# Two down projections as seven products of halves, with weight sums made in HBM and token sums made on VectorE

## The reference, cut to what matters

```python
def conv_ffn(x, w_up, conv_w, conv_b, w_down):      # x: (1, 512, 1024), D_FF = 2816
    up = x @ w_up
    a, g = up[..., :D_FF], up[..., D_FF:]
    g = causal_dwconv(g, conv_w) + conv_b
    return (jax.nn.gelu(g) * a) @ w_down             # (512 x 2816) @ (2816 x 1024)
...
x = layer_norm(alpha * x + conv_ffn(...), ln_ffn_g[layer], ln_ffn_b[layer])
```

## Time and profile before

| what | value |
|---|---|
| median of 3 runs | 1785.68 us (1784.17 to 1785.85) |
| profiled execution | 1786.04 us |
| its span, first to last instruction | 1784.2 us |
| PE busy | 1758.9 us, 99% of the span |
| PEld (weight loads, beside PE) | 1472.9 us, 83% |
| DVE busy | 1027.2 us, 58% |
| ACT busy | 652.2 us, 37% |
| POOL busy | 99.5 us, 6% |
| mean granted TensorE clock | 0.998 of full |
| HBM traffic | 189.67 MB, mean 106 GB/s |

### The profile page before, as it was taken

How to read it: one execution, slowest core, us unless ns; L and a number is a source line. 1 busy time by engine, 2 the same in 40 slices (tenths; PEclk the granted TensorE clock), 3 DMA queues, 4 the chain that set the end, 5 groups by cost and what they waited for, 6 DMA issues and landing times.

```text
span 1784.2 us, 27491 instructions
## 1 busy us (share of the span) xinstructions
PE 1758.9 (99%) x11571; PEld 1472.9 (83%) x11571; DVE 1027.2 (58%) x1480; ACT 652.2 (37%) x1013; POOL 99.5 (6%) x136
## 2 busy tenths in 40 slices
...
GB/s 302 111 94 113 113 49 77 147 95 102 98 95 107 94 83 128 109 95 117 108 107 60 89 195 153 142 154 130 138 94 36 151 60 73 38 38 63 176 36 83
DMA packets 146010, 189.67 MB, mean 106 GB/s; under 512 B 7800, under 2 KB 95092, under 8 KB 145120
## 3 DMA queue, kind: packets, MB, share of 16 engines
...
HBM read 181.58 MB, written 6.30 MB: 105 GB/s over the span
## 4 chain that ended last, share of the span: by engine, by line
PE 93%; DVE 4%; issue 1%; ACT 1%; POOL 1%; DMA 0%; SPq 0%; DVEq 0%; ACTq 0%
PE ps L329 28%; PE ps L331 27%; PE ps L330 27%; PE ps L970 2%; PE ps L518 1%; PE ps L2222 1%; PE ps L2242 1%; PE ps L1628 1%; PE ps L2236 1%; PE ps L2256 0%; DVE LATE L2303 0%; PE ps L2359 0%; PE ps L982 0%; DVE WL L313 0%; PE ps L1652 0%
## 5 line engine op out<-in xcount | busy, mean ns | idle before, releaser
L313 DVE TENSOR_TENSOR WL<-RAW,WH 128x1024 fp32r<-128x1024 f32 x289 | 350.8, 1223 | 501.3 <-ACT WH L303 500.0
L329 PE MATMUL ps<-XH,WH 128*128 128x512 f32 (+1 forms) x1416 | 524.6, 371 | 3.4 <-DVE XL L1498 1.6
L303 ACT ACTIVATE WH<-RAW 128x1024 fp32r<-128x1024 f32 x289 | 303.5, 1058 | 597.5 <-PE ps L331 570.0
L331 PE MATMUL ps<-XH,WL 128*128 128x512 f32 (+1 forms) x1416 | 518.2, 366 | 0.0
L330 PE MATMUL ps<-XL,WH 128*128 128x512 f32 (+1 forms) x1416 | 517.9, 366 | 0.0
L329 PE MATMUL ps<-WH,XH 128*128 128x512 f32 x784 | 312.7, 399 | 2.4 <-DVE WL L313 1.1
L329 PEld LDWEIGHTS ps<-XH,WH 128*128 128x128 f32 x1416 | 267.5, 189 | 51.4 <-issue 6.1
L331 PE MATMUL ps<-WH,XL 128*128 128x512 f32 x784 | 305.8, 390 | 0.0
L330 PE MATMUL ps<-WL,XH 128*128 128x512 f32 x784 | 305.5, 390 | 0.0
L331 PEld LDWEIGHTS ps<-XH,WL 128*128 128x128 f32 x1416 | 267.4, 189 | 43.4
L330 PEld LDWEIGHTS ps<-XL,WH 128*128 128x128 f32 x1416 | 267.7, 189 | 40.9
...
## 6 DMA issues: line engine op xcount, KB each, us to landing
RAW<-ffn_w_up SPq DMA_DIRECT2D x176, 256.0 KB, 3.2
RAW<-ffn_w_down SPq DMA_DIRECT2D x44, 512.0 KB, 3.7
RAW<-w_in SPq DMA_DIRECT2D x33, 512.0 KB, 3.9
RAW<-xa_wkv SPq DMA_DIRECT2D x32, 512.0 KB, 3.8
RAW<-c_w_in SPq DMA_DIRECT2D x24, 512.0 KB, 3.8
LATE<-w_ada SPq DMA_DIRECT2D x24, 512.0 KB, 4.8
RAW<-xa_wq SPq DMA_DIRECT2D x16, 512.0 KB, 5.7
RAW<-xa_wo SPq DMA_DIRECT2D x16, 512.0 KB, 3.7
```

The source lines that it names most:

```text
L303: e.activation(halves_of(i)[0][:, :, 0:w], raw(i)[:, :, 0:w], ACT.Copy).then_inc(*w_hi.up(i))
L313: e.tensor_tensor(wl[:, :, 0:w], raw(i)[:, :, 0:w], wh[:, :, 0:w].bitcast(F), ALU.subtract).then_inc(*w_lo.up(i))
L329: e.matmul(o, lh, rh, start=start, stop=False)
L331: return e.matmul(o, ll, rh, start=False, stop=stop)
```

## The change

With the features and the tokens cut in halves, the down projection is a product of 2 x 2 blocks. A11 and A21 are tokens 0 to 255 and 256 to 511 of features 0 to 1407, A12 and A22 the same of features 1408 to 2815; B00, B01, B10, B11 are the blocks of `w_down`. Strassen's scheme in Winograd's form makes it seven products of 256 x 1408 by 1408 x 512:

- product 1: A11 by B00; product 2: A12 by B10
- product 3: (A12 + s2) by B11; product 4: A22 by t4
- product 5: s1 by t1; product 6: s2 by t2; product 7: s3 by t3
- s1 = A21 - A22, s2 = s1 - A11, s3 = A11 - A21
- t1 = B00 + B01, t3 = B01 + B11, t2 = t3 + B00, t4 = t2 + B10, up to signs that are put right when the products are added

**Weight sums.** t1 to t4 of each layer are made in HBM (`d_sum`) by DMAs that POOL issues in `sums_pool`: for each sum a copy from HBM to HBM and then an accumulating DMA, each in two parts (6 and 5 feature tiles). Steps 0 to 5 are placed between stages: layer 0's step 0 before the four norms of the gating branch in `ab_pool`, then one step before and one behind the norms of "mix" and of "xa" in each layer, and step 5 before those of "ffn"; layer 1's step 0 follows layer 0's last norm.

**Token sums.** `token_sums` on DVE makes s3, s1 (in place of A21), s2 and A12 + s2 of each of 11 feature tiles, four operations of 128 x 256; nine of the eleven are inside the up projection, two in the down projection. `token_out` (POOL) writes s3, s2 and A12 + s2 to HBM (`d_tok`), and `token_in` (POOL) brings them back as needed into `ring`, two places of 128 x 512. A reload waits until the low part of the item two loads before it has been made.

**The order of the down projection.** 39 chunks and 40 token "items" of 128 x 512 per layer. Chunks 0 to 21 alternate a, a, b, b: a holds B00 and t1 (products 1 and 5), b holds t2 and t3 (products 6 and 7). Chunks 22 to 32 hold B10 and B11 (products 2 and 3), chunks 33 to 38 hold t4 (product 4). Items A are tiles of A11 with s1, B of s3 and s2, C of A12, D of A12 + s2, E of A22; B and D come through `ring`. Two 128-token tiles u = 0, 1 per product. Products 1, 5, 6 and 7 hold all eight PSUM banks; products 2 and 3 take the four banks of 1 and 5. DVE and ACT combine the products into `XR` in steps 20 to 28, and do the norm rows behind step 32. `early_pool` now stands behind `down_pool` on POOL's queue. The code, cut to its core:

```diff
+FAST = [(name, q + i) for q in range(0, 11, 2) for name in "ab" for i in range(min(2, 11 - q))]
+FAST += [("c", k) for k in range(11)] + [("e", q) for q in range(6)]
+def pair(q):
+    return min(2, 11 - 2 * q)
+def w_fast(l):
+    first["ffn", l] = len(chunks)
+    w = I["ffn_w_down"][l]
+    for name, k in FAST:
+        if name == "a":
+            chunks.append(([((0, 1), 512, w[128 * k:128 * k + 128, 0:512].unsqueeze(1)),
+                            ((1, 2), 512, d_sum[l][k][:, 2:3, :])], 512, ("t1", l, k)))
+        if name == "b":
+            chunks.append(([((0, 2), 512, d_sum[l][k][:, 0:2, :])], 512, ("t3", l, k)))
+        if name == "c":
+            chunks.append(([((0, 2), 512, w[1408 + 128 * k:1536 + 128 * k, :].rearrange("p (k n) -> p k n", k=2))],
+                           512, None))
+        if name == "e":
+            v = d_sum[l][2 * k:2 * k + pair(k)]
+            chunks.append(([((0, pair(k)), 512, v[:, :, 3, :].rearrange("k p n -> p k n"))], 512, ("t4", l, 2 * k + pair(k) - 1)))
...
+        if chunks[i][2] is not None:
+            what, l, k = chunks[i][2]
+            for name in (("t2", "t3") if what == "t3" else (what,)):
+                e.wait_ge(*sum_in[name][k // 6].at(l))
...
+        if nb == 9:
+            item_lo(e, l, 0)
+            item_lo(e, l, 1)
+        if nb > 6:
+            token_sums(e, l, 2 * nb - 13)
+        for c in range(4 if nb else 0):
+            if nb > 5 and c == 2:
+                token_sums(e, l, 2 * nb - 12)
+            if l:
+                side()
+            lo_to(e, first["up", l, nb] + min(c + 1, 3 if nb == 10 else 4) + NH)
+            if l:
+                side()
+        if nb < 10:
+            lo_to(e, first["up", l, nb] + 4 + NH)
+            for i in range(2):
+                conv_dve(e, l, nb, i)
+                gated_dve(e, l, nb, i)
+    conv_dve(e, l, 10, 0)
+    item_lo(e, l, 2)
+    conv_dve(e, l, 10, 1)
+    item_lo(e, l, 3)
+    gated_dve(e, l, 10, 0)
+    gated_dve(e, l, 10, 1)
+    lo_to(e, first["up", l, 10] + 4 + NH)
...
+    a11, a21, a12, a22 = hT[:, k, 0:256], hT[:, k, 256:512], hT[:, 11 + k, 0:256], hT[:, 11 + k, 256:512]
...
+    e.wait_ge(*ffn_v.at(("h", l, 11 + k)))
+    e.tensor_tensor(s3, a11, a21, ALU.subtract).then_inc(*ffn_v.up())
+    e.wait_ge(*latest["V"])
+    e.tensor_tensor(a21, a21, a22, ALU.subtract).then_inc(*ffn_v.up(("s1", l, k)))
+    e.wait_ge(*latest["V"])
+    e.tensor_tensor(s2, a21, a11, ALU.subtract).then_inc(*ffn_v.up())
+    e.wait_ge(*latest["V"])
+    e.tensor_tensor(last, a12, s2, ALU.add).then_inc(*ffn_v.up(("s", l, k)))
...
+    def part(name, g):
+        return d_sum[l][6 * g:6 + 5 * g, :, place[name], :].rearrange("k p n -> p k n")
+    def block(r, c, g):
+        return w[1408 * r + 768 * g:1408 * r + 768 + 640 * g, 512 * c:512 * c + 512].rearrange("(k p) n -> p k n", p=P)
+    def copied(name, g, src):
+        e.dma_start(part(name, g), src).then_inc(*sum_in[name][g].up((l, "copy")))
+    def added(name, g, src):
+        e.wait_ge(*sum_in[name][g].at((l, "copy")))
+        e.dma_start(part(name, g), src, accum_op=ALU.add).then_inc(*sum_in[name][g].up(l))
+    for g in range(2):
+        if step == 0:
+            copied("t1", g, block(0, 1, g))
+            copied("t3", g, block(0, 1, g))
+        if step == 1:
+            added("t1", g, block(0, 0, g))
+            added("t3", g, block(1, 1, g))
+        if step == 2:
+            e.wait_ge(*sum_in["t3"][g].at(l))
+            copied("t2", g, part("t3", g))
+        if step == 3:
+            added("t2", g, block(0, 0, g))
+        if step == 4:
+            e.wait_ge(*sum_in["t2"][g].at(l))
+            copied("t4", g, part("t2", g))
+        if step == 5:
+            added("t4", g, block(1, 0, g))
...
+def down_pool(e, l):
+    for i in range(2, 17):
+        token_in(e, l, i)
+        if i == 3:
+            token_out(e, l, 9)
+        if i == 7:
+            token_out(e, l, 10)
...
+def items_at(s):
+    got = [s + 8] if s < 14 else []
+    got += [ITEMS.index(("C", q)) for q, at in enumerate((2, 6, 10, 13, 16, 18)) if at == s]
+    got += [ITEMS.index(("D", q)) for q in range(6) if 14 + q == s]
+    return got + [ITEMS.index(("E", q)) for q, at in enumerate((20, 21, 23, 25, 27, 29)) if at == s]
...
 def down_pe(e, l):
...
+    for s, (name, k) in enumerate(ITEMS[0:22]):
+        e.wait_ge(*w_lo.at(i0 + s))
+        ready(s)
+        of = ((1, 0), (5, 256)) if name == "A" else ((6, 256), (7, 0))
+        for half, (p, at) in enumerate(of):
+            for u in range(2):
+                key = ("down", l, p, u)
+                if k == 0:
+                    ps.take(key)
+                    for w in ps.vacant(key):
+                        e.wait_ge(*w)
+                r = product(key, s, at + 128 * u, i0 + s, half, k == 0, k == 10)
...
+    for k in range(11):
+        i, mc = i0 + 22 + k, 22 + 2 * (k // 2)
+        e.wait_ge(*w_lo.at(i))
+        for half, p in enumerate((2, 3)):
...
+    for q in range(2):
+        for u in range(2):
+            last(q, u)
+    for u in range(2):
+        for q in range(2, 6):
+            last(q, u)
+            if (u, q) in ((0, 5), (1, 3)):
+                behind(u)
...
 def down_dve(e, l):
...
+    def row(t):
+        u = t % 2
+        if t < 2:
+            e.wait_ge(*gemm.at(("down", l, 2, u)))
+            e.wait_ge(*ln_v.at((n, "x11", u)))
+            add(2, t, 0)
+            stats_of(t, 0)
+            e.wait_ge(*gemm.at(("down", l, 3, u)))
+            e.wait_ge(*ln_v.at((n, "x12", u)))
+            add(3, t, 1)
+            stats_of(t, 1)
...
+    for s in range(33):
+        for u in range(2):
+            if s == 20:
+                e.wait_ge(*dn_a.at(("u", l, u)))
+                scaled(u, 0, U[u]).then_inc(*ln_v.up((n, "x11", u)))
+            if s == 21:
+                e.wait_ge(*gemm.at(("down", l, 6, u)))
+                e.wait_ge(*ln_v.at((n, "x11", u)))
+                e.tensor_tensor(U[u], U[u], ps.tile(("down", l, 6, u))[:, :], ALU.add).then_inc(
+                    *ps.empties(("down", l, 6, u), ln_v, (n, "sum", u)))
+                e.wait_ge(*ln_v.at((n, "sum", u)))
+                e.wait_ge(*gemm.at(("down", l, 5, u)))
+                e.tensor_tensor(Y[u], ps.tile(("down", l, 5, u))[:, :], U[u], ALU.subtract).then_inc(
+                    *ps.empties(("down", l, 5, u), ln_v, (n, "y", u)))
...
+        lo_to(e, min(i0 + s + 1 + NH, limit))
+        if s == 1:
+            token_sums(e, l, 9)
+        if s == 5:
+            token_sums(e, l, 10)
+        for m in items_at(s):
+            item_lo(e, l, m)
     for t in range(4):
+        if l == 0 and t == 2:
+            turn_dve(e, n, 0)
+        if l == 0 and t == 3:
+            lo_to(e, i0 + 36 + NH)
+        row(t)
+        if l == 0 and t == 2:
+            turn_dve(e, n, 1)
+        if l == 0 and t == 3:
+            lo_to(e, i0 + 37 + NH)
+        row_end(t)
+        if t < 2:
+            lo_to(e, min(i0 + 34 + t + NH, limit))
...
 def gpsimd(e):
...
+            if name == "mix":
+                sums_pool(e, l, 1)
+            if name == "xa":
+                sums_pool(e, l, 3)
+            if name == "ffn":
+                sums_pool(e, l, 5)
+                tokens_pool(e, l)
+                down_pool(e, l)
             if (name, l) == ("ffn", 1):
                 early_pool(e)
...
```

More of the change, by code:

```diff
@@ L245, in programs @@
             w_values(1, 0)
-        for b in range(2):
-            w_block(("ffn", l, b), I["ffn_w_down"][l], 512 * b, rows=DFF)
+        w_fast(l)
     for name, c0, n in (("k", 512, 512), ("w", 2048, 128), ("r", 0, 512), ("v", 1024, 512), ("aq", 2176, 512),
@@ L289, in programs @@
     c_a = sig("c_act", "A")
+    sum_in = {name: [sig(f"sum_{name}{g}", "dma", 16) for g in range(2)] for name in ("t1", "t2", "t3", "t4")}
+    tok_out, tok_in = sig("tok_out", "dma", 16), [sig(f"tok_in{i}", "dma", 16) for i in range(2)]
+    dn_a = sig("dn_a", "A")
     made = {"hi": 0, "lo": 0, "w": 0}
@@ new lines, in gated_dve @@
+    def gated_dve(e, l, nb, i):
+        j = 2 * nb + i
+        e.wait_ge(*ffn_a.at(("gelu", l, j)))
+        e.tensor_tensor(hT[:, j, :], gc[i], ps.tile((("up", l, nb), i))[:, :], ALU.mult).then_inc(
+            *ps.empties((("up", l, nb), i), ffn_v, ("h", l, j)))
+    ITEMS = [(name.upper(), k) for name, k in FAST if name in "ab"]
+    ITEMS += [(name, q) for q in range(6) for name in "CD"] + [("E", q) for q in range(6)]
+    ring = [big(11264 + 512 * i, 512) for i in range(2)]
+    LOADED = [("B", k) for k in range(11)] + [("D", q) for q in range(6)]
@@ new lines, in token_out, with token_in @@
+    def token_out(e, l, k):
+        pair_of, last = token_place(l)
+        e.wait_ge(*ffn_v.at(("s", l, k)))
+        e.dma_start(d_tok[l][k][:, 0:512], pair_of).then_inc(*tok_out.up())
+        e.dma_start(d_tok[l][k][:, 512:768], last).then_inc(*tok_out.up((l, k)))
+    def token_in(e, l, i):
+        name, k = LOADED[i]
+        if i >= 2:
```

(54 more changed lines are left out.)

349 lines of the change are left out of this document (224 added, 125 removed).

## The result

The changed kernel takes 1795.07 us (median of 4 runs, 1791.19 to 1797.52), the kernel before 1784.93 beside it (1784.11 to 1785.85): ratio 1.0056, 95% interval 1.0044 to 1.0067. It is slower by 0.56%, where I forecast 1777.8 us and faster. Its own runs lie 6.3 us apart, those of before 1.7.

What follows compares the result with a forecast made beforehand. PE, busy for 99% of the span, was taken to bound the kernel. Terms summed to -7.8 us: 1778.2 from the profiled 1786.04, or 1777.8 us against the median, 0.36 lower; forecast range 1771 to 1782.

Steps and rivals of the forecast that it cites:

- matmuls: Down projection: 66 fewer matmuls per layer at 0.2267 us each, -29.9 us in all.
- chunk 22, both layers: PE waits for product 3's banks (1.4 us) and late item D5 (0.6): +2.0 us per layer, +4.0.
- up to down, layer 1: Start of layer 1's down projection: B4's load, behind token sum 9's write, makes chunk 8 late, +2.5 us.
- end of layer 0: DVE's norm rows and low parts come late; PE waits 3.2, 3.5 and 0.5 us: +7.2 us.
- end of layer 1: Norm row 3 ends 12.9 us behind the last matmul, before 5.3: +7.6 us.
- clock, down projections: Half a clock dip of 1.6 us after PE's pauses at the end of layer 0: +0.8 us.
- weight sums: The DMAs in HBM, 16 per layer, cost zero, up to 2 us per layer if the cover fails.
- All stand stages ahead of their use ... zero: HBM weight-sum DMAs cost nothing: needed stages later, and down-projection weight loads have 8 us or more of reserve.
- One of my own signs of being wrong: The prediction is wrong if SP's weight loads land after 8 us.
- I take 4.2 ... D5 comes 0.6 us late: Token loads D1, D3, D5 land in 4.2 us; a turn takes 5.75 us, so D5 is 0.6 late before step 20.
- The ring rival: Token loads land slower than 4.2 us: 1794 at 6.2; chance 0.13 beyond 5.6, 0.14 for 4.7 to 5.6.
- It waits 0.7 and again 0.7: In chunk 22 PE waits twice for banks that DVE's step 21 frees: 1.4 us per layer.

Runs made afterwards that it cites:

- e1: Changed kernel with layer 1's weight-sum steps 4 and 5 issued ahead of the cross attention's norm, not behind it: 1787.25 us, ratio 1.0012.
- e9: Kernel before, products untouched, with the weight sums added at the changed kernel's places and read by nobody: 1794.21 us, ratio 1.0050.
- e10: Kernel before with the unread weight sums added, layer 1's steps 4 and 5 ahead of the cross attention's norm: 1787.07 us, ratio 1.0011.
- e2: Changed kernel with D items loaded into places free early, so that no D load waits for another D item: 1787.10 us, ratio 1.0014.
- e6: Changed kernel with e1's and e2's edits, B4's load before sum 9's write, ACT copying product 5, and layer 1's early loads held back: 1769.50 us, ratio 0.9913.
- e12: e6 plus last four chunks of products 2 and 3 by token tile, and layer 1's sum steps 2 to 5 moved earlier: 1760.26 us, ratio 0.9858.
- e11: e6 with POOL's order at B4 as in the changed kernel (write of token sum 9 ahead of B4's load): 1775.06 us, ratio 0.9941.

## Why the prediction was wrong

It was 17.3 us too low, 15.6 by the profiled executions, on which its sum was made (span 1784.2 to 1792.0). Term by term:

| term | predicted | measured |
|---|---|---|
| matmuls | -29.9 | -29.9 (132 fewer) |
| chunk 22, both layers | +4.0 | +9.5 (4.7 and 4.8) |
| up to down, layer 1 | +2.5 | +2.6 |
| end of layer 0 | +7.2 | +4.5 (1.7 and 2.8) |
| end of layer 1 | +7.6 | +6.2 |
| clock, down projections | +0.8 | about +5 (1.6, 1.8, 1.7) |
| weight sums | 0 | +7.5 |
| in no term | 0 | about +2.4 |
| sum | -7.8 | +7.8 |

**The step that failed first: "All stand stages ahead of their use ... zero".** I asked when the sums are needed, and whether the down weights have reserve, not what the sums delay while they run. My bound, 2 us where "the cover fails", was for weight loads of the down projection. In the up projection of layer 1, w_ada's loads already held the DMA engines at a share of 0.73 in 1020 to 1060, and that window of the trace before I had not read. e1, e9 and e10 settle it: the sums alone cost over 8 us, and their place accounts for most. One of my own signs of being wrong came with it: SP's weight loads landed after 15 us, past the 8 that I had named.

**"I take 4.2 ... D5 comes 0.6 us late".** The landing itself was well chosen for the later items of layer 1: median 4.0 us for the loads of 1300 to 1326, and from D3's low part to D5's high part took 5 us, as reckoned. And the chain lost little on its way: D0's high part came 5.5 us after it was due (behind the use of chunk 14, at 1309.3), D5's 6.0 us (chunk 19, 1322.9), so it grew by 0.5 where I had 0.6. But I let it begin on time. D0 and D1 were split 6.6 and 6.4 us behind their issue, while the loads of 1300 to 1326 together moved 302 GB/s, and B9, whose low part D0's load waits for, was itself split at 1306, where chunk 11 had been used by 1301.1. In layer 0 the 256 KB loads issued in 590 to 616 us had a median of 4.9, so there 4.2 was short too. The ring rival, at 1789 to 1794, thus came near the measured time, with the right place but the wrong mechanism (every landing slow): in e2 such loads landed later still (5.8 us in layer 0, 6.1 for those of 1290 to 1326), and only 0.7 us of waits was left in layer 0, because the D loads no longer waited for one another: D5's was issued by 602.1 us there, and at 612.68 in the changed kernel.

**"It waits 0.7 and again 0.7".** DVE's order was right, and with the ring free 0.7 us of it is seen in layer 0 (e2). I added the two lags, 1.4 and 0.6, as if the late item came once; but D5 delays ACT's copy and then DVE's whole order behind it, which is why taking out either one leaves only the other: 0.7 of 4.7 us in layer 0 (e2), 1.9 of 4.8 in layer 1 (e4).

**Clock.** I allowed one place. In fact each chunk 22 and the end of layer 0 had slow matmuls behind its waits, and a fourth stretch stood behind the modulation's wait (counted with the sums). The clock is a tax on waits: a pause of 3 us cost up to 1.8 more. In e6 and e12 the waits went and the slow stretches in the products with them. Not every wait had one behind it, and the length of the wait did not decide: 2.64 us at chunk 8 had none in the changed kernel, 2.46 us there had one in e11, and so had 1.89 us in e10. The rule of the Trainium skill that I cited ("TensorE: Matmul & The Clock Gate", the table under "Why this matters for your kernels"), to avoid idle gaps between bursts, is borne out by most of these rows. Had I priced every wait by the measured 1.6 to 1.8 us, my sum would have been some 4 us higher, by my estimate.

**Up to down** came to 2.6 for 2.5, in part by luck. My own times gave 24.7 less 21.8, so 2.9. B4's load, and the high part that waited for it:

```profile
1281.14 1.07 POOL L1394 DMA_DIRECT2D BIG<-token_sums  x2
...
1286.68 0.63 ACT L1462 ACTIVATE XH<-BIG 128x512 fp32r<-128x512 f32 x1 [8.69 <-DMA BIG<-token_sums]
```

PE wanted chunk 8 at 1287.45, so the up projection ended eight chunks before, at 1265.7. The load was issued 15.5 us behind that, where I had 17.0, and was split 5.5 us later, where I had 4.2. The two errors cancel but for 0.2.

**The ends** were right in mechanism, and 4.1 us cheaper together: the first transposes waited 1.7 for 3.2, the keys' block 2.8 for 4.0 (the profile puts that wait to issue, but PE went on at 677.04, 0.1 us after DVE's low part at L341 had ended). In layer 1 row 3 ended 25.8 us behind chunk 32 and not 27.9: row 0 began 0.7 earlier than I had it, and rows 2 and 3 came 5.0 us apart where I had 5.44.

What I can't place is the last 2.4 us: 0.43 us on a low part in each layer, matmuls behind a wait starting 0.3 us apart at first, some ten times 0.1, and the 1.1 gained at the start against them.
